# fp32 v, k and r in the time mix, and norms by pairs of rows with four units sharing each row

## The reference

```python
qkv = x @ w_in; ...differential attention, 8 heads...; o @ w_o        # attention
x = layer_norm(ALPHA * x + o, g, b)                                     # norm 0
x = layer_norm(ALPHA * x + (silu(x @ w_gate) * (x @ w_up)) @ w_down)    # FFN, 2816 wide; norm 1
# time mix (RWKV-7), six mixes of x with its neighbours
xs = x[None] + mu[0] * dx_prev[None] + mu[1] * dx_next[None]
r, k, v = einsum('ibld,ide->ible', xs[:3], w_rkv)
lw = tanh(xs[3] @ w1) @ w2;  decay = exp(-exp(-softplus(-(w0 + lw)) - 0.5))   # two directions
a  = sigmoid(a0 + (xs[4] @ a1) @ a2);  g = sigmoid(xs[5] @ g1) @ g2
kk = k * k_k, normalised per head of 64;  kd = k * (1 + (a - 1) * k_a)
y  = scan forward + scan backward over S = S*w - (S kk)(kk a)^T + v kd^T, y = S r
out = ((group_norm(y) + bonus) * g) @ w_o                               # rw_o
x = layer_norm(ALPHA * x + out)                                         # norm 2
x = layer_norm(ALPHA * x + moe_swiglu(x))      # 8 experts, top 2; norm 3
```

## Time and profile before

| | |
|---|---|
| median of 3 runs | 3032.13 us |
| the profiled execution | 3024.21 us, span 3022.4 us |
| mean granted TensorE clock | 0.937 |
| TensorE busy | 2725.1 us |
| VectorE busy | 2107.7 us |
| ScalarE busy | 1551.5 us |
| GpSimd busy | 87.0 us |

### The profile page before, as it was taken

How to read it: one execution, slowest core, us unless ns; L and a number is a source line. 1 busy time by engine, 2 the same in 40 slices (tenths; PEclk the granted TensorE clock), 3 DMA queues, 4 the chain that set the end, 5 groups by cost and what they waited for, 6 DMA issues and landing times.

```text
span 3022.4 us, 50549 instructions
## 1 busy us (share of the span) xinstructions
PE 2725.1 (90%) x21596; PEld 2247.3 (74%) x21596; DVE 2107.7 (70%) x2992; ACT 1551.5 (51%) x2209; POOL 87.0 (3%) x95
## 2 busy tenths in 40 slices
PE   8779998758797899999999999996999988999987
PEld 8558996658794666666666666664987978988977
DVE  4655546795434498898989889895676864666864
ACT  3433432422212287777777777773446444446443
POOL 0000000030000000000000000000000011000011
PEclk9669999879897799999999999998999999999999
DMA  6103552300003198999989899893334544334532
GB/s 211 56 15 112 173 171 93 94 1 4 3 4 122 61 369 332 351 348 348 350 333 367 332 348 352 331 367 99 105 112 127 157 128 147 113 104 127 159 125 98
DMA packets 244416, 547.71 MB, mean 181 GB/s; under 512 B 24492, under 2 KB 187784, under 8 KB 200924
## 3 DMA queue, kind: packets, MB, share of 16 engines
q1 hardware_dynamic: 242204, 541.54, 50.3%
q0 software_dynamic: 1984, 2.89, 0.3%
HBM read 540.46 MB, written 1.05 MB: 179 GB/s over the span
## 4 chain that ended last, share of the span: by engine, by line
PE 72%; DVE 16%; ACT 6%; issue 3%; DMA 2%; POOL 1%; DVEq 0%; SPq 0%; ACTq 0%; POOLq 0%
PE PS L158 19%; PE PS L160 18%; PE PS L159 18%; DVE wl L305 4%; ACT wh L296 3%; PE PS L969 1%; PE PS L382 1%; PE PS L2284 1%; PE PS L488 1%; PE PS L1729 1%; DMA raw<-in_w_in 1%; PE PS L997 1%; PE PS L371 1%; PE PS L1755 1%; PE PS L2256 1%
## 5 line engine op out<-in xcount | busy, mean ns | idle before, releaser
L305 DVE TENSOR_TENSOR wl<-raw,wh 128x1024 fp32r<-128x1024 f32 (+1 forms) x654 | 775.5, 1190 | 445.5 <-ACT wh L296 425.2
L296 ACT ACTIVATE wh<-raw 128x1024 fp32r<-128x1024 f32 (+1 forms) x654 | 670.7, 1028 | 632.2 <-PE PS L160 566.2
L305 DVE TENSOR_TENSOR wl<-early,wh 128x1024 fp32r<-128x1024 f32 x384 | 466.1, 1223 | 54.7 <-ACT wh L296 34.4
L296 ACT ACTIVATE wh<-early 128x1024 fp32r<-128x1024 f32 x384 | 407.0, 1061 | 126.9 <-PE PS L160 117.9
L158 PE MATMUL PS<-b_hn_h,wh 128*128 128x256 f32 (+2 forms) x1312 | 379.9, 290 | 26.3 <-DVE wl L305 9.6
L160 PE MATMUL PS<-b_hn_h,wl 128*128 128x256 f32 (+2 forms) x1312 | 371.6, 283 | 0.0
L159 PE MATMUL PS<-b_hn_l,wh 128*128 128x256 f32 (+2 forms) x1312 | 371.3, 283 | 0.0
L158 PE MATMUL PS<-wh,xe_h 128*96 128x512 f32 x896 | 356.8, 398 | 1.2 <-DVE xe_l L1881 1.2
L160 PE MATMUL PS<-wh,xe_l 128*96 128x512 f32 x896 | 353.2, 394 | 0.0
L159 PE MATMUL PS<-wl,xe_h 128*96 128x512 f32 x896 | 353.1, 394 | 0.0
L158 PEld LDWEIGHTS PS<-b_hn_h,wh 128*128 128x128 f32 (+2 forms) x1312 | 232.6, 177 | 31.7 <-issue 18.0
(11 more groups left out here) (498 smaller groups left out, 5331.0 us busy)
## 6 DMA issues: line engine op xcount, KB each, us to landing
early<-in_moe_in SPq DMA_DIRECT2D x128, 1024.0 KB, 4.8
raw<-in_moe_in SPq DMA_DIRECT2D x96, 1024.0 KB, 4.8
early<-in_moe_out SPq DMA_DIRECT2D x64, 1024.0 KB, 4.9
raw<-in_w_in SPq DMA_DIRECT2D x56, 1024.0 KB
raw<-in_moe_out SPq DMA_DIRECT2D x48, 1024.0 KB, 4.9
raw<-in_w_in SPq DMA_DIRECT2D x32, 704.0 KB
raw<-in_attn_w_in SPq DMA_DIRECT2D x12, 1024.0 KB, 5.8
raw<-in_rw_w_rkv SPq DMA_DIRECT2D x12, 1024.0 KB, 4.9
```

Source lines behind the costliest of these rows:

```text
L296: act.e.activation(st.two(n)[0], st.raw(n), ACT.Copy).then_inc(*act.sig("hi", st.name, n, sem=f"hi_{st.name}"))
L305: dve.e.tensor_tensor(lo, st.raw(n), hi.bitcast(F32), SUB).then_inc(*dve.sig("lo", st.name, n, sem=f"lo_{st.name}"))
```

## The change

1. v, k and r of the time mix are plain fp32: `unsplit_units` multiplies the raw slot's columns with the mix itself, a load of two units being freed by the second one's last matmul. Neither these pieces nor the mixes are split any more. v's units go in groups of four that share each row, k's in pairs, r's one by one. Loads come in the order v, w_lora, a_lora, k, g1, r.
2. The order on TensorE is v, lora_in w, lora_in a, lora_out w, k 0 to 3, lora_out a (with an input tile of its own, `rw_l2`), k 4 to 7, k_norm, gate_h, spread, r. VectorE makes `rw_e` in pairs of rows with mix 2 right behind, then mixes 3, 4, 1, 5, 0, both decays, k_k from PSUM, and BE, KE, kd, KA; RE x r is on VectorE too. ScalarE evacuates all of v, k and r; `k_part` (k_a a + 1 - k_a) is ScalarE's.
3. Norms: the sum's rows follow the residuals one by one. Centring, squares and var go in four pairs of rows. g times the reciprocal is one operation for each row, and ScalarE adds b into H (and in norm 0 into the high part too). Of the two busy streams one of five matmuls stays, after var. `down` no longer splits four pieces ahead.
4. `project_units`: the first four units share each row for qk, attn_o, gate and up (0 and 1), rw_o, iq and out. For rw_o these rows alternate with y_norm and y_gate.
5. RMS norms: squares in four pairs, with the sum's rows behind each; five busy matmuls after it in both layers.

```diff
-    projection(SA, "rv", A["rw_w_rkv"][0, 2], 0, D)
-    projection(SA, "k", A["rw_w_rkv"][0, 1], 0, D)
+    unsplit(SA, "rv", A["rw_w_rkv"][0, 2], 0, D)
     low_rank(SA, "w_lora", "rw_w1", "rw_w2")
     low_rank(SA, "a_lora", "rw_a1", "rw_a2")
+    unsplit(SA, "k", A["rw_w_rkv"][0, 1], 0, D)
...
+    def unsplit_units(pe, st, event, units, X, Tn, x_event=None):
...
+        for k in range(KC):
+            if x_event:
+                pe.wait_ge(pe.at(*x_event, k))
+            for i, m, b in zip(units, ms, bs):
+                c = i % 2 * 128
+                t = pe.e.matmul(PS[:, b, 0:Tn], cols_view(256)(st.slot(m))[:, k, c:c + 128], X[:, k, :], start=k == 0,
+                                stop=k == KC - 1)
+                if k == KC - 1:
+                    t.then_inc(*pe.sig("unsplit_mm", event, i))
+                    pe.also(event + ".mm", i)
+                    if i % 2:
+                        pe.also("direct", st.name, m)
+
+    def project_units(pe, st, event, items, X, Tn, x_event, banks=None):
...
+        for k in range(KC - 2):
+            pe.wait_ge(pe.at(*x_event, k))
+            for event, i, b, before, n, w in taken:
+                row(k, b, w)
+            yield
+        for event, i, b, before, n, w in taken:
+            for k in range(KC - 2, KC):
+                pe.wait_ge(pe.at(*x_event, k))
+                t = row(k, b, w)
+            t.then_inc(*used(pe, st, n))
...
     def norm_pe(pe, key, after, Tn=T):
+        for k in range(KC):
+            pe.wait_ge(pe.at(after, k))
+            t = pe.e.matmul(PS[:, b, 0:Tn], ones, H[:, k, 0:Tn], start=k == 0, stop=k == KC - 1)
...
+        for k in range(KC):
+            pe.wait_ge(pe.at("ln_sq", key, k // 2))
+            t = pe.e.matmul(PS[:, b, 0:Tn], ones, LNQ[:, k, 0:Tn], start=k == 0, stop=k == KC - 1)
+        t.then_inc(*pe.sig("ln_mm", key, "var"))
+        busy_pe(pe, 5, key)
...
+        for k in range(KC):
+            e.scalar_tensor_tensor(LNQ[:, k, :], H[:, k, :], par("ln_g", key * 8 + k), LNR, MUL, MUL).then_inc(
+                *dve.sig("ln_scaled", key, k))
+            if x and k:
+                low_of(k - 1)
...
+        for u in (0, 4):
+            unsplit_units(pe, SA, "rv", range(u, u + 4), MIXED[2], T, ("mixed", 2))
...
+        lora_in("w_lora", 3)
+        lora_in("a_lora", 4)
+        lora_out("w_lora", rw_l)
+        for u in (0, 2):
+            unsplit_units(pe, SA, "k", range(u, u + 2), MIXED[1], T, ("mixed", 1))
+        lora_out("a_lora", rw_l2)
+        for u in (4, 6):
+            unsplit_units(pe, SA, "k", range(u, u + 2), MIXED[1], T)
...
+        for f in range(KC + 2):
+            if f >= 2:
+                next(first_units, None)
+            if f >= KC:
+                continue
+            b, before = bank("y_norm", f, b=f % 2)
...
+        for i in (3, 4, 1, 5, 0):
+            for k in range(KC):
+                mix(i, k)
...
-        pool.wait_ge(pool.at("exp", 0, "re"))
+        pool.wait_ge(pool.at("prep", 1, "ka"))
         pool.wait_ge(pool.at("r", 7))
-        pool.wait_ge(pool.at("r", 6))
-        e.tensor_tensor(RE[0], RE[0], rw_r, MUL).then_inc(*pool.sig("prep", 0, "re"))
...
     def rms_pe(pe, l):
-        pe.wait_ge(pe.at("rms_sq", l))
         for k in range(KC):
+            pe.wait_ge(pe.at("rms_sq", l, k // 2))
...
+        for _ in project_units(pe, SB, "iq", [("iq", (l, u)) for u in range(4)], (hh, hl), SEQ, ("x_lo", f"hn{l}")):
+            pass
```

More of the change, by code:

```diff
@@ L374, in norm_pe @@
     def norm_pe(pe, key, after, Tn=T):
[L376 to L384, removed]
@@ new lines, in norm_pe, with norm_act @@
+        if before:
+            pe.wait_ge(pe.at(*before))
+        for k in range(KC):
[3 more added lines that the diff above has]
+        busy_pe(pe, 5, key)
+    def norm_act(act, key, hi=None):
+        for c in range(4):
+            r = slice(2 * c, 2 * c + 2)
+            act.wait_ge(act.at("ln_centred", key, c))
+            act.e.activation(flat(LNQ[:, r, :]), flat(H[:, r, :]), ACT.Square).then_inc(*act.sig("ln_sq", key, c))
@@ L398, in norm_dve @@
+    def norm_dve(dve, key, x=None):
+        e = dve.e
+        for c in range(4):
+            r = slice(2 * c, 2 * c + 2)
+            dve.wait_ge(dve.at("ln_mm", key, "sum"))
+            e.scalar_tensor_tensor(H[:, r, :], bc(ps("ln_sum", key), [128, 2, T], 1), -1.0 / D, H[:, r, :], MUL, ADD).then_inc(
+                *dve.sig("ln_centred", key, c))
+        dve.also("ln_sum", key)
         dve.wait_ge(dve.at("ln_mm", key, "var"))
@@ L873, in lora, with lora_out @@
             t.then_inc(*pe.sig("lora_mm", key))
+        def lora_out(key, x):
+            m = SA.of[key]
+            w2v = SA.slot(m)[:, D:2 * D]
             pe.wait_ge(pe.at("lora_h", key))
@@ L1079, in rwkv_pe @@
         pe.wait_ge(pe.at("y_var_r"))
-        for f in range(KC):
-            b, before = bank("y_norm", f)
+        first_units = project_units(pe, SA, "rw_o", [("rw_o", i) for i in range(4)], po_y, T, ("x_lo", "rw_o"),
+                                    (4, 5, 6, 7))
+        for f in range(KC + 2):
[4 more added lines that the diff above has]
+            b, before = bank("y_norm", f, b=f % 2)
             pe.wait_ge(pe.at(*before))
@@ L1266, in evacuated @@
-        def evacuated(what, dst, u):
-            dve.wait_ge(dve.at(what + ".mm", u))
-            e.tensor_copy(dst[:, u, 0:T], ps(what, u)).then_inc(*dve.sig(what, u))
-        dve.wait_ge(dve.last)
+        for k in range(0, KC, 2):
+            r = slice(k, k + 2)
+            dve.wait_ge(dve.at("h", 1, k + 1))
+            e.tensor_tensor(rw_e[:, r, 1:T], H[:, r, 0:T - 1], H[:, r, 1:T], SUB)
+            e.tensor_scalar(rw_e[:, r, 0:1], H[:, r, 0:1], -1.0, None, MUL)
+            e.tensor_copy(rw_e[:, r, T:T + 1], H[:, r, T - 1:T]).then_inc(*dve.own())
+            dve.wait_ge(dve.last)
+            mix(2, k)
+            mix(2, k + 1)
@@ L1285, in rwkv_dve @@
-        mix_with(1, KC)
-        for u in range(8):
-            if u < 4:
-                low(dve, SA)
-            mix(3, u)
-            if u % 2 == 0:
-                evacuated("k", rw_k, u)
-        for k in range(KC):
-            mix(4, k)
-        dve.wait_ge(dve.at("k", 7))
-        dve.wait_ge(dve.last)
-        for f in (0, 4):
-            e.tensor_tensor(rw_kk[:, f:f + 4, 0:T], rw_k[:, f:f + 4, 0:T], bc(par("k_k", f, 4), [128, 4, T], 2), MUL).then_inc(
-                *dve.sig("k_k", f))
@@ L1299, in rwkv_dve @@
-        for k in range(KC):
-            mix(5, k)
-        for n in range(2):
-            low(dve, SA)
-        dve.wait_ge(dve.at("k_norm_mm"))
-        e.tensor_scalar(n16, ps("k_norm", p=16), 1e-24, None, MAX).then_inc(*dve.sig("k_norm"))
-        for n in range(2):
-            low(dve, SA)
-        for k in range(KC + 1):
-            mix_with(0, k)
-            if k == 1:
-                dve.wait_ge(dve.at("k_norm_root"))
-                e.reciprocal(r16, n16).then_inc(*dve.sig("k_norm_r"))
+        e.tensor_scalar(less_ka, par("k_a", 0, 8), -1.0, 1.0, MUL, ADD).then_inc(*dve.sig("less_ka"))
@@ L2357, in second_pe @@
             projected(pe, l, "out_a", u, oT)
-        for u in range(KC):
-            projected(pe, l, "out", u, (q_r, k_r), ("m_lo", l) if u == 0 else None)
+        for _ in project_units(pe, SB, "out", [("out", (l, u)) for u in range(4)], (q_r, k_r), SEQ, ("m_lo", l)):
+            pass
+        for u in range(4, KC):
+            projected(pe, l, "out", u, (q_r, k_r))
         if l:
```

297 lines of the change are left out of this document (144 added, 153 removed).

## The result

The changed kernel takes 2982.07 us (median of four runs, 2978.38 to 2985.74) against 3031.38 for the kernel before (median of four, 3027.84 to 3035.63): a ratio of 0.984, 95% interval 0.9821 to 0.9859. The forecast was 2954 with a range of 2926 to 2984; the median lies 2 us inside its end, and two of the four executions (2985.02 and 2985.74) lie outside. The profiled execution has a span of 2983.9 us against 3022.4, so the two traces account for 38.5 us; the rest of the 49 is that the execution profiled before was a short one and the one after a long one of its kernel.

What follows compares the result with a forecast made beforehand. TensorE was busy 90% of the span; the forecast sought stretches it doesn't bound, with VectorE setting the end before the scan. 13 + 8.7 + 24 + 0 + 9 + 7 + 20 - 3.7 = 78 off 3024.2, plus 7.9: 2954 us, range 2926 to 2984.

Steps and rivals of the forecast that it cites:

- Norms: Sums behind residuals and work in pairs of rows gain 13 us in norm 0, 8.7, 9 and 7 in norms 1 to 3.
- Second blocks: Earlier sums, shared units of iq and out, and the last rms gain 20 us, bounds 12 and 24.
- Time mix: From norm 1's reciprocal to the scan's first forward matmul, 163 us against 188; 24 us gained.
- RE x r stands on VectorE now ... two products of half size (2 x 1.2): End of the time mix: behind r's last row only these products and masks remain, forward at R + 163.
- Gated output and rw_o: Rows of rw_o among y's steps: 7 us lost at low clock or 5 gained if it rises; taken as 0.
- the cases in which it rises: The y stage at full clock: alone (2949, chance 0.06) or with lora_out a's banks free in time (2934, chance 0.11).
- rival 2: Time mix: more stalls by loads waiting for slots freed in groups, 20 us, 2974; chance 0.14.
- Rival 1: Clock lost behind the shortened busy streams at five places, 14 us, 2968; chance 0.12.
- Rival 3: Time mix: fp32 v, k and r run at the lower clock throughout, 84 us lost, 3038; chance 0.04.
- Rival 4: Gated output: the y stage rises to full clock with its denser work, 5 us, 2949; chance 0.06.
- rival 6: Nothing moves: TensorE's added 19 us and new waits eat all of the gain, 3030; chance 0.03.
- Rival 5: lora_out a's banks are free in time and the y stage rises too, 20 us, 2934; chance 0.11.

Runs made afterwards that it cites:

- Unshared: The changed kernel with gate and up (0 and 1), iq and out one unit after the other again; span 2984.3 us, ratio 0.9865 to the kernel before.
- y banks: The changed kernel with y's eight steps in a row, rw_o's units behind them, PSUM bank numbers kept as in the changed kernel; span 2959.2 us, ratio 0.9787.
- y apart: The changed kernel with y's eight steps in a row, rw_o's units behind them, banks taken in turn again; span 2961.3 us, ratio 0.9813.
- Bonus late: The changed kernel with GpSimd's three bonus products waiting for VectorE's last RE x r; span 2978.8 us, ratio 0.9814.
- y lag: The changed kernel with rw_o's shared rows three steps behind y instead of two; span 2977.9 us, ratio 0.9809.
- y wide: y banks with the narrow matmuls of y's steps replaced by ones of 128 rows, leaving out part of the computation; span 2942.6 us.
- no busy: The changed kernel without the streams of five busy matmuls (both calls of `busy_pe` left out); span 2994.9 us, ratio 0.9888.
- exponentials later: The changed kernel with ScalarE's second exponentials behind the squares of k 0 to 3 and lora a's sigmoids; span 2975.7 us, ratio 0.9825.
- y lag 2: The kernel of y lag, unchanged, run once more for the trace of another execution; 2975.13 us.

## Why the prediction was right, and by how much it was wrong

**Norms: right.** The start and both norms were forecast to bring 18.0 us at norm 1's R and brought 18.1; R at 465.48 and gate's first four units on time. The router came 9.9 us earlier instead of 9. From norm 2 to norm 3's R 2.6 us came instead of 7: of norm 3's own 19.9 us from the first residual to R, 4.2 went, and the router's matmuls took 6.5 instead of 5.1 us, as they are now paced by the rows.

**Second blocks: right in sum (19.7 for 20), wrong in kind.** I gave most of it to shared units. Unshared shows 1.6 to 1.8 us a layer for iq, and 0.4 in the blocks as a whole. No run takes the rest apart into the squares in quarters, the sums behind them and the busy matmuls. And some of it is none of these: between iq's last matmul and out_a's first, where nothing was edited, the two layers took 4.4 us less. In the kernel before, out_a of the first layer waits for `b_m`:

```profile
2509.34 0.55 PE L158 MATMUL PS<-b_o,wh 128*128 128x256 f32 x1 [3.82 <-DVE b_m L2727]
```

In the changed kernel this wait is gone, as in y banks, and in y apart, with other bank numbers, it is there again. The change renumbers the banks of these blocks, and the forecast had no term for that. That the sum came out at 19.7 for 20 is in part luck.

**Time mix: the mechanism right, one term mis-sized.** v's first row, the wait for v's fourth load (4.64 for 4), lora_out a as the place that waits for ScalarE's exponentials (ended at R + 92 for R + 91, though it idled 7.82 us instead of 14 and its matmuls then took 8.3 us, at a granted clock of 0.50), k's third load behind it (5.76 for 5), r's end (R + 162 for 158) stood as the steps had them. The term that was wrong is "RE x r stands on VectorE now ... two products of half size (2 x 1.2)". I took away GpSimd's products beside VectorE's and forgot that the bonus products stand on GpSimd behind the same event, r's last unit. Bonus late measured that: 9.4 us. With the 4 us by which r ended late, it makes up the 13 us that the stage fell short. Bonus late also shows that moving GpSimd's work moves the collision into the scan (one product of 3.70 us); what it costs there isn't shown.

**Gated output and rw_o: this is the step that failed.** I put it at 0, between 7 us lost and 5 gained, and it lost 24. By the changed kernel's rows:
- six interleaved rows at 2.7 us and the last two of each unit from 955.1 to 959.9 are 21.1 us at mostly half clock; the same 96 matmuls took 12 before: 9.1.
- seven waits for a low part: 6.7. I had not looked at what the row's own input waits for. VectorE makes low part f only behind gate f + 1, so two steps of lag were one too few. y lag took these away, and its stage was 6.0 us shorter.
- the third load, 7.6. I wrote that it "still follows y", and then gave it no price. Before, it was hidden behind four units of 3 us that came after y; the change moved these units ahead of y's end and took the cover away.
- the last four units, which start at the low clock: 14.2 us, where the first four before, which did so too, took 13.9. 0.4.

23.8 in all, of 24.1, for this execution. That the clock wouldn't rise with denser work was rightly doubted there, from the row of 28.09 busy us in 28.10. I still gave 0.17 in all to the cases in which it rises. The Trainium skill (TensorE: Matmul & The Clock Gate, Part 1) says that the throttled state is the default and that activity releases it. Whoever takes busy time for activity expects this stage at full clock; y lag was busy for 47.7 of 48 us at 0.50, so the measurement decides against that reading, and y wide was at 1.00 from 908 us on.

**The total: in the range, by luck in part.** The two stages above took 37 of the 78 us away, and 2982 against 2954 is outside my own narrower bounds, 2940 to 2968, to which I had given half of the chance. The wider range held it by 2 us because it had room for other failures (rival 2), not because it priced the gated output.

**The rivals.** Rival 1 (the clock is lost behind shortened busy streams) didn't happen after norm 0 and in iq, where the granted clock was 1.00, and no busy shows that the five left are worth having. In v the first rows ran at 0.50, but v's did so in the kernel before as well, behind the longer stream (second line), so the shortening isn't the cause there:

```profile
470.91:473.50 2.59, 2.59 (x6) 2.01 (x7) 2.48 (x8) 0.00 (x0) 0.00 (x0) 0.50 0.34 131
497.00:500.00 3.00, 2.49 (x8) 1.85 (x9) 2.90 (x8) 0.86 (x2) 0.00 (x0) 0.50 0.15 48
```

Rival 2 (2974) came nearest in size, by a cause that was only a small part of the loss: the waits for v's fourth and k's third load were within 0.8 us of the forecast. Rival 3 is out: r's matmuls took 0.49 us. Rival 4, the y stage at full clock, is out, at 0.53, and rival 6, no gain, by the ratio. Rival 5 needed the banks of lora_out a free, and exponentials later shows what they were worth, 7 us.

## What to carry to other kernels

Work put between the steps of a stage that runs at half clock can run at half clock too, as it did here for most of the stage, and it no longer covers what it covered behind the stage; price both, and the row's own inputs, before taking such an edit at nothing. When an operation leaves GpSimd, look at what GpSimd does next and who waits for the same event. Where buffers are numbered in turn over a whole program, fix the numbers before you compare two orders, or a stage far away moves as well, here by 9.4 us, and its gain or loss is put down to the edit.

## What the runs showed of the hardware that I had not expected

TensorE can be busy without a break for 48 us at a granted clock of 0.50 (1.2 GHz) when part of its matmuls are narrow: y lag, whose steps have two matmuls of 16 rows, one of 32 and one of 128, with twelve more of 128 rows ahead of each of the last five steps. In y lag 2 and in the executions with two steps of lag the clock rose now and then for some microseconds, to a mean of 0.52 to 0.60. With 128 rows in all matmuls (y wide), they went from 0.91 to 0.46 us apart within the second step, and the eight steps from 28.1 to 13.5 us. VectorE's products of two SBUF tensors took up to 5.97 us instead of 1.29 next to GpSimd's, the last two each ending 1.2 us behind the end of one of GpSimd's; in the kernel before, products twice as large ended 2.3 us behind. So the price here was what was left of GpSimd's instruction, and not a share of a rate.
